# Moving the start of three matmul operands by 64 or 128 bytes in a two-block transformer kernel

## What is computed

```python
def swiglu(h, w_in, w_out):
    g, u = jnp.split(h @ w_in, 2, axis=-1)
    return (jax.nn.silu(g) * u) @ w_out
...
    y_x = merge_heads(na_latent(q_x, k_x, v_x, k_c, v_c, rpb))
...
        h = rmsnorm(x, norm1_g[i])
        z = h @ w_in[i] + b_in[i]
...
        merged = jax.nn.sigmoid(gm) * (y_m @ w_bm[i]) + jax.nn.sigmoid(gr) * (y_r @ w_br[i])
        x = x + merged @ w_out[i]
...
        h2 = rmsnorm(x, norm2_g[i])
        x = x + jnp.square(jax.nn.relu(h2 @ w_ff1[i] + b_ff1[i])) @ w_ff2[i] + b_ff2[i]
...
        h3 = rmsnorm(x, norm3_g[i])
        x = x + jax.nn.sigmoid(h3 @ w_pe_gate[i]) * (p[i] @ w_pe[i])
```

## Time and profile before

| | |
|---|---|
| median of three runs | 2325.57 us |
| profiled execution, its own time | 2333.59 us |
| span of the profiled execution, first to last instruction | 2331.4 us |
| instructions | 32818 |
| PE (TensorE matmul) busy | 2247.9 us, 96% |
| PEld (TensorE weight load) busy | 1935.4 us, 83% |
| DVE (VectorE) busy | 1481.7 us, 64% |
| ACT (ScalarE) busy | 1021.3 us, 44% |
| mean granted TensorE clock | 0.986 |
| HBM traffic | 166 GB/s over the span |

### The profile page before, as it was taken

One profiled execution on the slowest core, in us unless ns is written; L12 is line 12 of the kernel. 1 busy time (PEld: TensorE's weight loads), 2 busy tenths in 40 slices (PEclk: granted clock), 3 DMA queues, 4 the chain that ended last, 5 costly groups with the idle time before them and its releaser, 6 DMA issues.

```text
span 2331.4 us, 32818 instructions
## 1 busy us (share of the span) xinstructions
PE 2247.9 (96%) x14070; PEld 1935.4 (83%) x14070; DVE 1481.7 (64%) x1878; ACT 1021.3 (44%) x1238; POOL 27.7 (1%) x52
## 2 busy tenths in 40 slices
PE   6998989999997999999999999999999999999997
PEld 3775667777786878999989877999999988789997
DVE  4787543333445567655788767685678876768576
ACT  4256341121224346443565345454466634445444
POOL 0000000000000000000000000000000000000000
PEclk9999989999998999999999999999999999999998
DMA  8540135444423252455565554555547555455552
GB/s 331 199 163 1 43 122 197 162 191 170 162 92 109 93 140 73 163 182 198 205 231 197 180 185 146 181 198 187 193 174 250 186 182 202 148 174 188 188 193 108
DMA packets 56504, 389.97 MB, mean 167 GB/s; under 512 B 6688, under 2 KB 7080, under 8 KB 11176
## 3 DMA queue, kind: packets, MB, share of 16 engines
q1 hardware_dynamic: 51848, 370.56, 43.7%
q0 software_dynamic: 4512, 17.31, 2.6%
HBM read 386.79 MB, written 1.06 MB: 166 GB/s over the span
## 4 chain that ended last, share of the span: by engine, by line
PE 81%; DVE 11%; ACT 4%; issue 2%; DMA 2%; SPq 0%; DVEq 0%; ACTq 0%
PE PS L514 25%; PE PS L515 24%; PE PS L516 24%; DVE w_lo L1688 2%; DMA raw<-chunks_in 2%; PE PS L838 1%; PE PS L1013 1%; ACT w_hi L1215 1%; PE PS L992 1%; PE PS L717 1%; PE PS L677 1%; DVE BIG L2297 1%; ACT xn L1293 1%; PE PS L742 1%; DVE PS L1908 1%
## 5 line engine op out<-in xcount | busy, mean ns | idle before, releaser
L1688 DVE TENSOR_TENSOR w_lo<-raw,w_hi 128x2048 fp32r<-128x2048 f32 x300 | 684.9, 2290 | 505.5 <-ACT w_hi L1215 502.8
L1215 ACT ACTIVATE w_hi<-raw 128x2048 fp32r<-128x2048 f32 x300 | 573.0, 1915 | 760.8 <-PE PS L516 441.4
L514 PE MATMUL PS<-x_hi_lo,w_hi 128*128 128x256 f32 (+1 forms) x2112 | 639.6, 303 | 9.5 <-DVE x_hi_lo L1753 5.2
L515 PE MATMUL PS<-x_hi_lo,w_lo 128*128 128x256 f32 (+1 forms) x2112 | 636.8, 302 | 0.0
L516 PE MATMUL PS<-x_hi_lo,w_hi 128*128 128x256 f32 (+1 forms) x2048 | 611.6, 299 | 0.0
L514 PEld LDWEIGHTS PS<-x_hi_lo,w_hi 128*128 128x128 f32 x2112 | 399.8, 189 | 36.4 <-issue 18.6
L515 PEld LDWEIGHTS PS<-x_hi_lo,w_lo 128*128 128x128 f32 x2112 | 400.0, 189 | 16.6
L516 PEld LDWEIGHTS PS<-x_hi_lo,w_hi 128*128 128x128 f32 x2048 | 388.7, 190 | 14.2
L514 PE MATMUL PS<-w_hi,x_hi_lo 128*128 128x512 f32 (+1 forms) x800 | 318.6, 398 | 16.1 <-DVE x_hi_lo L1753 11.9
L516 PE MATMUL PS<-w_lo,x_hi_lo 128*128 128x512 f32 (+1 forms) x800 | 315.0, 394 | 0.0
L515 PE MATMUL PS<-w_hi,x_hi_lo 128*128 128x512 f32 (+1 forms) x800 | 314.3, 393 | 0.0
(11 more groups left out here) (316 smaller groups left out, 2153.3 us busy)
## 6 DMA issues: line engine op xcount, KB each, us to landing
raw<-chunks_in SPq DMA_DIRECT2D x348, 1024.0 KB, 4.8
bias_ring<-brows_in POOLq DMA_DIRECT2D x32, 256.0 KB, 4.1
G<-nrows_in POOLq DMA_DIRECT2D x2, 1536.0 KB, 9.8
BIG<-rel_in POOLq DMA_DIRECT2D x4, 512.0 KB, 7.3
free_b<-rel_in POOLq DMA_DIRECT2D x4, 512.0 KB, 8.4
tabt<-tabs_in SPq DMA_DIRECT2D x1, 1280.0 KB, 10.4
X<-x_in SPq DMA_DIRECT2D x1, 1024.0 KB, 8.5
X<-ctx_in SPq DMA_DIRECT2D x1, 1024.0 KB, 10.5
```

The costliest lines, as they stand in the source:

```text
L514: pe.matmul(o, lhs[0], rhs[0], start=start, stop=False, **more)
L515: pe.matmul(o, lhs[1], rhs[0], start=False, stop=False, **more)
L1215: act.activation(w_hi[:, i % HI_RING, :], ring[:, n % RING, :], ACT.Copy).then_inc(*hi_ready.now(n))
L1688: dve.tensor_tensor(w_lo[:, c % RING, :], ring[:, c % RING, :], w_hi[:, i % HI_RING, :].bitcast(F32), ALU.subtract).then_inc(*lo_ready.now(c))
```

## The change

Both constants become 16 floats (64 bytes) smaller, and `yT_na` begins at `X_AT` instead of at 0. The offset of x and of the feed-forward input becomes 128 bytes in place of 192, that of the attention output 128 in place of 0. The four engines that compute and SP have the same instructions in the same order; no size, wait or transfer differs. Operands of the stages with 512 tokens, and the weight slots, stay.

```diff
-X_AT = 112
-FF_AT = 48
+X_AT = 96
+FF_AT = 32
...
-        yT_na = pair_of((xhi_[:, 0:2048], xhi_[:, 2048:4096]), 256, 8)
+        yT_na = pair_of((xhi_[:, X_AT:X_AT + 2048], xhi_[:, X_AT + 2048:X_AT + 4096]), 256, 8)
```

## The result

The change makes the kernel slower. Its median is **2361.1 us** (2359.2 to 2363.1, five runs) against 2325.6 before: ratio 1.0142, 95% interval 1.0124 to 1.0160, so +33 us by the ratio, with an interval of about 29 to 37. The forecast was 2309.

The account below looks back on a forecast made before the run. PE's matmul pace was taken to bound the kernel. Terms of -10.6 (x and feed-forward input), -1.3 (attention output) and -4.6 (stationary x) gave -16.5 us, from 2325.6 to 2309; full range 2285 to 2360.

Parts of the forecast that it names:

- That starts modulo 256 set the pace, and the counts: 256-column matmuls lose 7 to 13 ns each by operand starts; 7056 at offset 192, 2406 of them at the slow 117.7.
- I take the fast rhythm for all of it, 113.3: 256-column matmuls on x and feed-forward input, offset 192 to 128: 10.6 us saved; bounds +36.7 and 38.8 saved.
- Attention output: 192 matmuls of w_out, offset 0 to 128: from 120.0 to 113.3 ns each, 1.3 us saved.
- Stationary x: 1536 matmuls streaming 512 weight columns past x: 226.7 ns each, 4.6 us saved; bounds 5.5 lost, some 15 saved.
- Writers: ScalarE and VectorE writing x 64 bytes lower, and moved small tiles: costed at 0, with 1 us either way.
- History: In 256-column streams at offset 192, only what ran before a stretch tells its two paces apart, 113.3 and 117.7 ns.
- Rival A: Offset 128 counts as 0, collision repeating every 128 bytes: all 7056 matmuls at 120.0 ns, +32.1, so 2357.7 us; chance 0.33.
- B: Slow rhythm everywhere in the 256-column streams: 20.5 us lost, less 4.6 and 0.4, so 2341 us; chance 0.07.
- C: Collision of operand reads goes away altogether: 109.3 ns for 256 columns, -45.5 us, so 2280; chance 0.10.
- D: No effect: new starts have the same two rhythms in about the same shares, 2325 to 2328 us; chance 0.10.
- The difference alone explains little: Gate matmuls: stationary starts from 0 to 112 bytes, moving start at 64, yet 512 columns take 230 ns throughout.
- The 8 us: Median 8.0 us below the profiled execution's 2333.6, perhaps because fewer stretches fell into the slow rhythm; taken over unchanged.

Follow-up runs that it names:

- micro3: Streams alone, no transformer: start differences 192, 128 and 64, each with ten different lead-ins; 192 ran at 113.3 ns in six cases, 117.8 in four.
- off64: Kernel before the change, with x, feed-forward input and attention output all at offset 64: 2353.7 us, ratio 1.0116.
- micro2: Streams alone, no transformer: start differences in finer steps, 8 bytes at 256 columns and 16 at 512; nothing below 113.3 ns at 256 columns.
- yt192: Kernel before the change, with only the attention output moved, from offset 0 to 192: 2326.5 us, ratio 0.9998.
- padded kernels: Kernel before the change, with 64 or 128 unused bytes ahead of the whole arena, all start differences kept: 2328.8 us (1.0002) and 2327.9 us (1.0012).
- slots: Kernel before the change, with chunks streamed past stationary x moved to difference 0 and attention output to offset 192: 2329.3 us, ratio 1.0006.
- x_only: Kernel before the change, with only x moved, from offset 192 to 128: 2355.2 us, ratio 1.0122.
- ff_only: Kernel before the change, with only the feed-forward input moved, from offset 192 to 128: 2341.3 us, ratio 1.0064.

## Why the prediction was wrong

- **What bounds the kernel**: right. The changes of time were changes of pace in PE's streams, less up to 5 us of PE's waits.
- **That starts modulo 256 set the pace, and the counts**: right. The step that failed is "I take the fast rhythm for all of it, 113.3". Measured over about 7200 matmuls at offset 128: 119.0 ns. In place of 10.6 us saved by that term, 28 us were lost (4.0 x 7056), within its upper bound of +36.7. The prediction took offsets for a smooth curve with its worst at 0 and its best opposite. The table is neither smooth nor symmetric: 192 is a single good value, and 64, just as far from 0, has 117.8 in every stretch of the kernel.
- **Attention output**: -1.3 forecast, 192 x (118.7 - 120.0) = -0.2 measured.
- **Stationary x**: the prediction took 226.7 because both starts are multiples of 128 again. It is 232.4: +4 us in place of -4.6. The bound of 233.3 held, but "nothing else in it is worth 5 us" did not: this term was 8.6 us off.
- **Writers**: cost nothing that shows; DVE and ACT are busy 1483.0 and 1021.5 us after, 1481.7 and 1021.3 before.
- **History**: that it picks between the two rhythms of offset 192 fits micro3 and the kernels. That the weight loads bear out a collision of two reads was not: they last 188 ns at 118.7 as at 113.3.
- **Rival A** had nearly the number, 2357.7, by the wrong mechanism, which is luck. It said that the collision repeats every 128 bytes, which off64 and the tables refute, and that 512-column streams would return to 226.7. They went to 232.4 (8.6 us above its sum), which cancels what 118.7 in many stretches saved against its 120.0 (7056 x 1.0, 7.1 us). Rivals B, C and D fell: neither 117.8 nor anything below 113.3 occurs at 128.
- **The difference alone explains little**, as rival A read from the gate matmuls, was wrong too. They step the start by 16 bytes, and in micro2 such steps at 512 columns cost 231.7 to 234.7 ns but at differences 0 and 64. An average of 230 over eight of them says nothing against the difference.
- **The 8 us** between the profiled execution and the median fit the slow rhythm, as supposed: its 256-column mean was 115.0 ns, that of yt192 and the padded kernels 114.0, and 7056 x 1.0 is 7 us, all of it in the feed-forward from 937 us on. So about 7 of the 10.6 us of the first term weren't there to save in the median.

The range of 2285 to 2360 ended 1.1 us short. With rival A at 0.33 it should have reached past 2357.7 by more than the spread of the runs, some 5 us.

## What to carry to other kernels

When TensorE is bound by a stream in which every matmul loads its own weights, measure the pace (difference of starts) for each pair of starts modulo 256 in a kernel of streams alone, which costs one run; don't work out one offset from its neighbours. Here moving minus stationary of 192 bytes was best for 256 fp32r columns and 0 for 512, and moving x by 64 bytes cost 1.2%, the feed-forward input 0.6%. The table by itself isn't a forecast either: moving one stream can put the next into its slower pace, as slots, x_only and ff_only did. Gains of 4 to 8 us can't be claimed from one profile of such a kernel: compare medians of many runs.

## What the runs showed of the hardware

- fp32r streams with a weight load for each matmul run at a few exact paces, with all other engines idle: most at 113.3, 117.8, 118.7 or 120.0 ns for 256 columns, and at 226.7, 228.9, 232.4 or 233.3 for 512 (starts in steps of 64).
- The pace goes by the difference of the two starts modulo 256 bytes, and steps of 8 bytes change it: 113.3 or 117.8 at 192 became 120.0 at 184 and at 200.
- One pair can have two paces, and a stream keeps the one that it has fallen into. Which one is mostly set by the program and not by chance: in the profiles of four kernels every stretch but one has the same rhythm in all four, and moving a neighbouring stream's start changed it (x_only, ff_only, slots). With other engines idle offset 192 ran at 113.3 after one matmul of 512 columns and at 117.8 after three, each seen once.
- Why 192 takes 113.3 in most cases and 64 in one of all those measured stays open: the runs give the table, not the mechanism behind it.
